# Holding back one 2 MB weight load until two gathers of token rows have landed

## What is computed

```python
N_GROUPS, E_PER_GROUP, TOP_K, D_EXPERT = 4, 8, 2, 256      # 32 experts

def _hier_moe(h, w_rg, b_rg, w_re, b_re, w_gate, w_up, w_down):
    ...                                    # top-1 group, then top-2 experts in it -> gates (tokens, 32)
    out = jnp.zeros_like(xt)
    for e in range(N_EXPERTS):
        he = jax.nn.silu(xt @ w_gate[e]) * (xt @ w_up[e])
        out = out + gates[:, e:e + 1] * (he @ w_down[e])
    return out.reshape(b, t, d)

# for context and for latent tokens:
x = x + gt1 * _rmsnorm(token_mix(...), g_post1)
h = _modulate(x, g_pre2, sh2, sc2)
x = x + gt2 * _rmsnorm(_hier_moe(h, ...), g_post2)
```

## Time and profile before

| what | value |
|---|---|
| median of 3 runs | 689.76 us |
| the 3 runs | 689.76, 1586.45, 688.75 us |
| the profiled execution | 688.46 us |
| its span, first to last instruction | 686.5 us |
| TensorE matmul / weight load busy | 586.2 / 346.6 us |
| VectorE / ScalarE / GpSimd busy | 267.3 / 155.8 / 70.6 us |
| moved by DMA | 173.35 MB, mean 253 GB/s |

### The profile page before, as it was taken

One profiled execution on the slowest core, in us unless ns is written; L12 is line 12 of the kernel. 1 busy time (PEld: TensorE's weight loads), 2 busy tenths in 40 slices (PEclk: granted clock), 3 DMA queues, 4 the chain that ended last, 5 costly groups with the idle time before them and its releaser, 6 DMA issues.

```text
span 686.5 us, 9558 instructions
## 1 busy us (share of the span) xinstructions
PE 586.2 (85%) x3831; PEld 346.6 (50%) x3831; DVE 267.3 (39%) x455; ACT 155.8 (23%) x323; POOL 70.6 (10%) x95
## 2 busy tenths in 40 slices
PE   0899999999999999999999765989899899688810
PEld 0766666555555455544545653455455455355400
DVE  2414999999745434403334540111011110011117
ACT  3310000012416444422223420101101101010125
POOL 5000000300000000000000025121111111110001
PEclk9999999999999999999999987999999999999975
DMA  9999955000004570019112960799999999999959
GB/s 333 342 369 401 411 187 200 14 0 1 1 0 153 224 296 11 1 50 379 61 62 93 413 281 23 290 380 420 423 424 424 422 423 423 424 426 422 386 232 274
DMA packets 47636, 173.35 MB, mean 253 GB/s; under 512 B 5738, under 2 KB 12235, under 8 KB 35290
## 3 DMA queue, kind: packets, MB, share of 16 engines
q1 hardware_dynamic: 39856, 158.47, 57.7%
q0 software_dynamic: 6448, 12.54, 5.5%
q10 hardware_dynamic: 1274, 1.52, 0.6%
HBM read 162.79 MB, written 17.06 MB: 262 GB/s over the span
## 4 chain that ended last, share of the span: by engine, by line
PE 66%; DMA 15%; SPq 6%; DVE 4%; ACT 3%; issue 2%; another core or an unknown queue 2%; ACTq 0%; DVEq 0%; POOLq 0%
PE ps L1501 14%; DMA arena<-in_w_up 11%; PE ps L1745 10%; PE ps L1878 9%; SPq L500 5%; PE ps L1894 5%; PE ps L1506 4%; PE ps L1502 4%; PE ps L1565 3%; PE ps L1519 3%; PE ps L1704 3%; PE ps L1737 3%; PE ps L1691 2%; DMA x<-in_x_sample 2%
## 5 line engine op out<-in xcount | busy, mean ns | idle before, releaser
L1878 PE MATMUL ps<-arena 128*64 128x256 f32 x992 | 116.8, 394 | 13.0 <-DMA arena<-in_w_up 5.1
L1501 PE MATMUL ps<-arena 128*128 128x512 f32 x216 | 111.1, 596 | 0.7 <-issue 0.6
L1878 PEld LDWEIGHTS ps<-arena 128*64 128x64 f32 x992 | 76.0, 143 | 57.2 <-issue 15.9
L1164 DVE SCALAR_TENSOR_TENSOR arena<-arena 128x655 f32<-128x655 f32 x116 | 95.9, 906 | 0.4 <-issue 0.2
L1506 PE MATMUL ps<-cst,arena 128*128 128x128 f32 (+2 forms) x349 | 52.2, 298 | 27.0 <-DVE arena L1103 17.3
L1745 PE MATMUL ps<-arena 128*128 128x512 f32 x160 | 69.7, 593 | 1.9 <-DVE arena L1275 1.0
L1894 PE MATMUL ps<-arena 128*64 128x512 f32 x256 | 58.5, 598 | 14.9 <-ACT arena L1006 14.8
L1502 PEld LDWEIGHTS ps<-arena 128*128 128x128 f32 x216 | 41.0, 190 | 51.6 <-issue 51.6
L1506 PEld LDWEIGHTS ps<-cst,arena 128*128 128x128 f32 (+2 forms) x349 | 44.3, 178 | 37.8 <-issue 27.5
L1444 DVE TENSOR_TENSOR arena<-arena,ps 128x256 f32<-128x256 f32 x16 | 6.7, 422 | 121.5 <-ACT arena L1035 121.5
L1745 PEld LDWEIGHTS ps<-arena 128*128 128x128 f32 x160 | 30.0, 190 | 38.1 <-issue 37.0
(11 more groups left out here) (284 smaller groups left out, 600.0 us busy)
## 6 DMA issues: line engine op xcount, KB each, us to landing
arena<-in_w_up SPq DMA_DIRECT2D x15, 2048.0 KB, 24.5
arena<-in_w_down SPq DMA_DIRECT2D x15, 2048.0 KB, 25.6
arena<-in_w_gate SPq DMA_DIRECT2D x14, 2048.0 KB, 24.8
arena<-in_w_ada SPq DMA_DIRECT2D x12, 2048.0 KB, 13.9
arena<-y_d SPq DMA_DIRECT2D x10, 512.0 KB, 7.2
arena<-in_w_out SPq DMA_DIRECT2D x1, 4096.0 KB, 13.7
arena<-ada_d SPq DMA_DIRECT2D x8, 512.0 KB, 8.1
x<-in_w_gate SPq DMA_DIRECT2D x2, 2048.0 KB, 26.0
```

The source lines that it names most:

```text
L1164: ins = dve.scalar_tensor_tensor(dst, src, w, dst, ALU.mult, ALU.add)
L1501: mm(pp(name)[:, 0:TS], lhs(k), rhs_s(k), start=k == 0, stop=k == steps - 1)
L1878: last = mm(ps[a:a + ROWS, s, n * FE:(n + 1) * FE], src[:, k, a:a + ROWS], w[:, j, k * FE:(k + 1) * FE], start=k == 0, stop=k == KD - 1)
```

## The change

Before the load of piece 9, SP now also waits until the first two gathers (the rows of pairs 0 and 1) have landed. Nothing else is changed.

```diff
             sp.wait_ge(x_st, 16 * NT)
+
+            for s in range(2):
+                sp.wait_ge(xg_in[s], 16)
             load(9)
 
             sp.wait_ge(cnt_ready, 1)
```

## The result

| | median | runs |
|---|---|---|
| before | 689.42 us | 10 |
| changed | 686.52 us | 10 |
| ratio | 0.9949, 95% interval 0.9934 to 0.9964 | |
| profiled execution of the changed kernel | 683.97 us, span 682.0 us | 1 |

What follows compares the result with a forecast made beforehand. The prediction took the DMA-rate-limited weight stream, started by piece 10's issue, as the bound. The start moves 3.2 us to 3.9 + 1.7 = 5.6 us earlier; taking 4.5, 689.76 - 4.5 = 685.3 us, range 681.8 to 690.0 us.

Steps and rivals of the forecast that it cites:

- What bounds the kernel: Weight stream, about 450 to 640 us: DMA rate limits it, so the end follows piece 10's issue at 432.66 us.
- Why the gather took 7.95 us: First gather, issued at 399.41 us: what it meets in the DMA queues is piece 9, 2.10 MB.
- (a): SP's two added waits: cost 0, as piece 9 fits the idle DMA gap; 5 us without that gap.
- (b): First gather on empty queues takes 2.8 us; transposes start 3.9 us earlier, bounds 0 to 4.0 us.
- the drain: Last PSUM buffer before the transposes, drained at 403.32 us: expected to be late next, capping the gain at 4.0 us.
- (c): TensorE's clock in transposes and first gate and up matmuls: without the idle time up to 1.7 us more, lower bound 0.
- (d): Pair 0's two unknown waits before the further round: earlier gains come through, or only 3.2 us if GpSimd's scatters set it.
- (e): Further round's gather, now beside piece 9: lands between 408.5 and 417.6 us, taken as 412 us, covered by matmuls.
- My even share: Further round's gather and piece 9 sharing DMA engines evenly: the gather would lose only 1.2 us; the sum didn't use it.
- The first: Rival, chance 0.13: no effect that counts, gather late for other reasons or unknown waits have their own time; 689 us.
- The second: Rival, chance 0.09: slower, piece 9 delays the further round's gather to 417.6 us, both unknown waits behind it; 690.5 us.
- The third: Rival, chance 0.12: larger gain, the unknown 4.5 us before pair 0's silu are missed too; 680.8 us.

Runs made afterwards that it cites:

- variant 5: The kernel before, with GpSimd's ten scatters of token numbers and the reading back of these lists left out: 679.96 us, ratio 0.9857.
- variant 7: variant 4 with GpSimd's ten scatters and the reading back of the lists left out: 674.21 us, ratio to before 0.9779.
- variant 9: variant 4 with the scatters and the reading back behind a branch, taken only if some expert needs a third round: 675.08 us, ratio to before 0.9771.
- variant 1: The changed kernel with piece 9 held back further, until directly before piece 10, past the idle DMA gap: 690.74 us, ratio to before 1.0024.
- variant 3: The changed kernel with pieces 5 and 8 also held until the first two gathers have landed: 686.66 us, ratio to before 0.9958.
- variant 4: The changed kernel with piece 9 held back until TensorE is through with pair 0's gate half: 686.57 us, ratio to before 0.9963.
- variant 8: variant 4 with GpSimd's ten scatters moved behind its gather for pair 3, nothing left out: 684.04 us, ratio to before 0.9907.
- variant 2: The kernel before with piece 9 held only until the counts are ready, with no wait for a gather: 687.47 us, ratio 0.9976.
- variant 6: The changed kernel with GpSimd's ten scatters and the reading back of the lists left out: 679.41 us, ratio to before 0.9839.
- variant 10: The changed kernel with each of the ten scatters replaced by a plain store to a fixed place: 679.66 us, ratio to before 0.9860.
- variant 11: The changed kernel with each scatter issued only after the one before has landed: 692.72 us, ratio to before 1.0045.

## Why the prediction held, and what was off

The direction, the range and the mechanism were right; the size was 3.5 us where I had said 4.5. Point by point, by the prediction's own parts:

- **What bounds the kernel.** Right. The end followed the issue of piece 10, 3.75 us against 3.3 us from the gather's issue, and the stream ran at 423 GB/s on either side. In variants 5, 7 and 9 too an earlier piece 10 came through to the end.
- **Why the gather took 7.95 us.** Right. With piece 9 away it took 4.25 us.
- **(a)** Right, and shown from the other side: in the gap piece 9 costs nothing, outside it 5.2 us (variant 1).
- **(b)** Mis-sized a little. I priced the gather at the shortest of 17, 2.8 us, and that one brings two rows, not a hundred (variant 3). A pair's gather takes 3.9 us alone, and the first of two took 4.24 to 4.41 us in variants 1, 3, 4, 7 and 8 as well. The gather, not the drain, stayed what the transposes waited for, and they start 4.46 us from its issue where I had 4.1: a gain of 3.54 us for 3.9.
- **(c)** Right in itself: the clock stayed at 2.4 GHz, the transposes took 1.12 us for 1.99 and the matmuls 7.13 for 7.7. But here it came to nothing, since the step behind it was waiting for something else. What piece 10 gained beyond the copy's 3.12 us is 0.63 us in the further round's 64 matmuls (8.56 us for 9.19), and I can't credit that to the change: with the same early start they took 8.45 to 9.88 us in variants 1 to 4.
- **(d)** This is where the missing 1 us went. I had two ends, 3.2 us if the scatters set the middle and 5.6 us if not, and took a value between them, as if there were something in between. There was one mechanism, the scatters', and it was the lower end: the copy moved by 3.12 us from the gather's issue, the scatters by 3.20 us. Variants 4, 5 and 7 show it. That my 4.5 us came within 1 us of the 3.5 us is in part luck: it was a mean of two mechanisms, of which only one was there.
- **(e)** I took 412 us for the further round's rows; they came at 414.1 us, 9.7 us from the gather's issue. The cover that hid the price was not only the matmuls, as I wrote, but mostly the hold-up by the scatters. Without it the collision costs 4.1 us (variants 6 and 7) and the change is worth 1.2 us, which its interval doesn't part from nothing. My even share was wrong twice. It priced 0.52 MB, where this gather brings 8 KB and should by such a share lose next to nothing; it took 9.06 us in variant 6 and 9.40 us in variant 10. And the Trainium skill ("DMA: Bandwidth & Descriptors", Queues, rings and completion order) says only that a DMA engine drains a whole packet from one queue before it goes to the next, not that the bytes are shared evenly. How much of piece 9 one turn takes, no run here shows.
- **The rivals.** The first is refuted by the ratio's interval. The second had its mechanism, not its size: TensorE had its rows 9.7 us from the gather's issue, and 11.3 us would decide. The third (the unknown wait before the silu vanishes) did not happen here; variant 5 shows that this wait and the one before the copy were worth up to 9.9 us together.

## What to carry to other kernels

Before a transfer that everything waits for, count the bytes that are queued ahead of it; a load that nobody needs soon belongs in the next idle stretch of the DMA engines. But look for who is issued in that stretch: the load only changes its victim, and that it costs nothing may be owed to another stall. And where the chain shows an unknown wait, line its end up against every other engine's last instruction in several runs before pricing what lies ahead of it: here the unknown wait was worth three times the change.

## What the runs showed of the hardware

- **Back to back small scatters by GpSimd go with late counts from TensorE.** While ten indirect scatters of 128 four-byte numbers each are issued 1.3 us apart, what waits for TensorE (a silu, a copy) starts 4.5 to 10.6 us after TensorE's own records say that the work is done, and the last such step 2.8 to 3.4 us after the start of the tenth scatter, in six kernels. TensorE's semaphore counts are themselves recorded that late (410.90 and 421.44 us in variant 4). With ten plain stores, with scatters one at a time, or with none, the silu follows at once. Later in the kernel the same ten scatters stretch 64 matmuls from 7.1 to 13.6 us (variant 8). In the first place TensorE's matmul records show no stall, only its counts and those who wait do. Why it happens no run here shows.
- **A gather fares badly beside a bulk load, however small it is.** A gather of two rows (8 KB) takes 2.8 us on nearly idle queues and 9.0 to 9.4 us beside a single 2.10 MB load (variants 6, 10 and 11), hardly more beside three (9.2 us to TensorE's start). One of some 100 rows (0.4 MB) takes 3.9 us alone, 4.2 to 4.4 us with a second right behind it, and 8.0 to 8.2 us when piece 9 is queued ahead (kernel before, variant 5).
- **A short idle time of TensorE can be paid twice, but need not be.** After 2.39 us without work (variant 6) the next 64 matmuls took 10.07 us at a granted clock of 0.70. After 2.30 us (variant 11) they took 7.13 us at 1.00, as where there was no such idle time (variant 7). What parts the two no run here shows.
